# Hybrid encoder layer with a mixture of experts: units of the second expert loaded into tiles that the mix stage leaves

## The reference

```
logits = hf @ w_router + b_router            # top 4 of 32, softmax over the 4
hm = xblk @ w_mlp1[e] + b_mlp1[e]            # 1024 x 2048 weights
act = gate * sigmoid(1.702 * gate) * (up + 1)  # gate and up are clamped
y = act @ w_mlp2[e] + b_mlp2[e]              # 1024 x 1024 weights
x = x + sum over the chosen experts of weight * y ; out = rmsnorm(x, g_final)
```

## Time and profile of the kernel before

| what | us |
|---|---|
| three executions, median (lowest to highest) | 1252.73 (1252.02 to 1252.94) |
| the profiled execution, its own time | 1250.43 |
| its span, first to last instruction | 1248.6 |
| TensorE busy (93% of the span) | 1164.3 |
| VectorE, ScalarE, GpSimd busy | 361.7, 196.0, 23.8 |
| chain that ended last: TensorE, DMA | 55%, 41% |
| bytes moved | 445.25 MB, mean 357 GB/s |

### The profile page before, as it was taken

The page is one execution under the profiler, slowest core; times in us unless marked ns, Lnnn a source line. Parts: engine busy times, 40 slices in busy tenths (PEclk is TensorE's granted clock), DMA queues, the critical chain, the costliest instruction groups (busy, mean ns, idle before and its releaser), DMA issues.

```text
span 1248.6 us, 17054 instructions
## 1 busy us (share of the span) xinstructions
PE 1164.3 (93%) x6731; PEld 583.3 (47%) x6731; DVE 361.7 (29%) x1018; ACT 196.0 (16%) x383; POOL 23.8 (2%) x35
## 2 busy tenths in 40 slices
PE   9999999999999999989998989989899989999996
PEld 7888888889433333333333333333333333333332
DVE  4505788121522212212221222122222222222112
ACT  2121344001311011111101000100110111010002
POOL 0001011000000000000000000000000000000000
PEclk9999999999899999999999999999999999999999
DMA  9944323447699999999999999999999999999995
GB/s 310 311 135 135 105 98 102 173 147 290 252 416 430 426 428 427 427 428 428 428 428 428 428 429 428 429 428 428 428 428 428 428 428 429 429 428 427 427 426 231
DMA packets 69555, 445.25 MB, mean 357 GB/s; under 512 B 6247, under 2 KB 43595, under 8 KB 44651
## 3 DMA queue, kind: packets, MB, share of 16 engines
q1 hardware_dynamic: 65976, 441.99, 86.2%
q10 hardware_dynamic: 3539, 2.69, 0.7%
HBM read 443.62 MB, written 1.05 MB: 356 GB/s over the span
## 4 chain that ended last, share of the span: by engine, by line
PE 55%; DMA 41%; ACT 1%; issue 1%; DVE 1%; ACTq 0%; SPq 0%; POOL 0%; DVEq 0%
DMA ring<-in_w_mlp_dram 41%; PE bank L735 25%; PE bank L483 14%; PE bank L486 4%; PE bank L730 3%; PE bank L717 2%; PE bank L782 1%; PE bank L615 1%; PE bank L605 1%; PE bank L459 1%; PE bank L577 1%; PE bank L645 1%; ACT arena L1070 1%; PE bank L724 1%; PE bank L706 0%
## 5 line engine op out<-in xcount | busy, mean ns | idle before, releaser
L735 PE MATMUL bank<-ring,arena 128*64 128x512 f32 x3072 | 689.0, 597 | 56.8 <-DMA ring<-in_w_mlp_dram 55.1
L735 PEld LDWEIGHTS bank<-ring,arena 128*64 128x64 f32 x3072 | 209.6, 137 | 487.1 <-issue 367.9
L1448 DVE TENSOR_TENSOR arena<-bank,b1T 128x256 f32<-128x256 f32 x128 | 53.8, 421 | 599.6 <-PE bank L782 597.3
L483 PE MATMUL bank<-hT,ring 128*128 128x256 f32 x544 | 119.4, 379 | 0.0
L483 PEld LDWEIGHTS bank<-hT,ring 128*128 128x128 f32 x544 | 103.2, 190 | 14.0
L1067 ACT ACTIVATE arena<-bank 128x512 f32<-128x512 f32 x32 | 19.1, 597 | 362.3 <-PE bank L735 362.2
L730 PE MATMUL bank<-arena 64*128 64x512 f32 x256 | 63.6, 615 | 0.8 <-ACT arena L1079 0.8
L486 PE MATMUL bank<-ring,hT 128*128 128x256 f32 x288 | 63.8, 380 | 0.0
L486 PEld LDWEIGHTS bank<-ring,hT 128*128 128x128 f32 x288 | 54.2, 190 | 7.1
L717 PEld LDWEIGHTS bank<-slotP,hb 128*128 128x128 bf16 x1488 | 45.1, 98 | 23.5 <-issue 23.5
L782 PE MATMUL bank<-cst,arena 128*128 128x128 f32 x256 | 40.5, 286 | 13.2 <-ACT arena L1067 8.4
(11 more groups left out here) (229 smaller groups left out, 659.7 us busy)
## 6 DMA issues: line engine op xcount, KB each, us to landing
ring<-in_w_mlp_dram SPq DMA_DIRECT2D x190, 2048.0 KB, 32.7
ring<-in_w_in_dram SPq DMA_DIRECT2D x24, 1024.0 KB, 11.5
ring<-in_w_br_attn_dram SPq DMA_DIRECT2D x4, 1024.0 KB, 5.0
ring<-in_w_br_ssm_dram SPq DMA_DIRECT2D x4, 1024.0 KB, 5.1
ring<-in_w_out_dram SPq DMA_DIRECT2D x4, 1024.0 KB, 5.2
ring<-in_w_mlp_dram SPq DMA_DIRECT2D x4, 1024.0 KB, 33.9
xres<-in_x_dram SPq DMA_DIRECT2D x2, 512.0 KB, 4.5
cst<-shape_constants_dram ACTq DMA_DIRECT2D x1, 608.0 KB, 13.1
```

The source lines that it names most:

```text
L483: last = nc.tensor.matmul(o, w[:, k, a * P:(a + 1) * P], rhs[:, k, :], start=(k == 0), stop=(k == KD - 1))
L735: return nc.tensor.matmul(bank[b][side * CAP:(side + 1) * CAP, :], tokens, w, start=start, stop=stop, skip_group_check=True)
L1448: step(V.tensor_tensor(o, side(bank[b][:, :]), bias_h.to_broadcast([P, 4, CAP]), ALU.add))
```

## The change

Four units of the second expert, numbers 16 to 19 (its fifth to eighth), go to tiles outside the ring: 16 to `mix_only` (a new name for 8 KB per partition over constants and small tiles of the mix stage, which are put side by side for it), 17 to `hN`, 18 to `hT`, 19 to `xres`. `hb3` leaves `hT` for the arena. The two pairs after them (units 20 to 23) take the ring's first two places and are loaded as single units, each after its own slot's use. The first gather is cut in three: two tokens' slices, two more, and the other four between the second and third unit. Bias products and the token weights' transposes go from expert 0 to expert 28, all residual rows into the first expert and before it, g_final is loaded as one row and spread by a product with ones in expert 29, a one-column sigmoid stands ahead of ScalarE's loop, the last slot transposes move between up units, and each token tile is stored by one 512 KB transfer.

```diff
@@ tiles
+        mix_only = sb("mix_only", [P, UNIT], at=place_of["cst"] + 4 * C_GE)
...
+        gfin = arena[:, 2048:3072]
+        b2s = arena[0:NE, 2048:3072]
+        grow = arena[NE:NE + 1, 2048:3072]
+        hb3 = sb("hb3", [P, TT, D], BF16, at=place_of["arena"] + 4 * 3584)
+        lastWT = arena[:, 9536:9792]
+        AWAY = {16: mix_only[:, :], 17: hN[:, :, :].rearrange("p t d -> p (t d)"),
+                18: hT[:, :, :].rearrange("p k l -> p (k l)"), 19: xres[:, :, :].rearrange("p t d -> p (t d)")}
+HALVED = (PAIRS + 2, PAIRS + 3)
+        def turn(g, first):
+            return g - 2 if g >= PAIRS or not first else g
+        def pair_at(g, first=False):
+            return PAIR_ORDER[turn(g, first) % PAIRS]
@@ SP's queue
+            sp.wait_ge(y_psum, KD)
+            load_away(16)
+            for g in range(PAIRS):
+                first_free(pair_at(g, True))
+                load_first(g)
+            sp.wait_ge(unit_done, N_MIX)
+            load_away(18)
+            sp.wait_ge(lg_psum, 1)
+            load_away(17)
+            for g in HALVED:
+                p = pair_at(g, True)
+                for h, done in ((0, pair_full[p]), (1, half_full[HALVED.index(g)])):
+                    unit_used(sp, 0, 2 * (turn(g, True) - PAIRS) + h)
+                    sp.dma_start(ring[:, 2 * p + h, :], half_src(g // EXP_PAIRS, g % EXP_PAIRS, h)).then_inc(done, 16)
+            for g in range(HALVED[-1] + 1, BODY * EXP_PAIRS):
+                t = turn(g, True) - PAIRS
+                unit_used(sp, 0, 2 * (t + (2 if t >= PAIRS else 0)) + 1)
+                load_first(g)
+                if t == KD // 2 - 1:
+                    sp.wait_ge(rows_done, 1)
+                    sp.wait_ge(hb_ready, 1)
+                    sp.wait_ge(res_ready, 1)
+                    sp.wait_ge(away_full, 16 * 3)
+                    load_away(19)
...
+            for t in range(TT):
+                sp.wait_ge(fin_ready[2 * t], 1)
+                sp.wait_ge(fin_ready[2 * t + 1], 1)
+                sp.dma_start(out[0, t * P:(t + 1) * P, :], hN[:, t, :]).then_inc(out_done, 16)
@@ TensorE
             rows_in_sums(1, 1)
+            rows_in_sums(2, 0)
...
+            def first_expert():
+                pe.wait_ge(pw_ready, 1)
+                for q in range(KD):
+                    if q in (0, 2):
+                        pe.wait_ge(x0_ready, 1 + q // 2)
+                    if q == 2:
+                        first_gather(4, KD, 3).then_inc(x_psum, 1)
+                    if q == 4:
+                        pe.wait_ge(x32_ready, 1)
+                    up_unit(0, 0, q, body0=True)
+                rows_in_sums(2, 1)
+                pe.wait_ge(hs_ready, 1)
+                transposes(0).then_inc(t_psum, 1)
+                pe.wait_ge(hs_ready, 2)
+                transposes(1).then_inc(t_psum, 1)
+                pe.wait_ge(route_ready, 1)
+                rows_in_sums(3, 0)
+                rows_in_sums(3, 1).then_inc(rows_done, 1)
+                pe.wait_ge(hb_ready, 3)
+                pe.wait_ge(p_ready, 2)
+                gather(1, 3).then_inc(x_psum, 1)
+                down_units(0, 0, body0=True)
...
+            def expert(i, c, final=False, body0=False, bias_too=False, gain_too=False):
...
+                    if bias_too and q == 1:
+                        pe.wait_ge(late_in, 16 * 3)
+                        weights_T()
+                    if bias_too and q in (3, 5):
+                        bias_products(q // 4)
+                    if gain_too and q in (1, 3):
+                        gain_rows(q // 2)
+                    if final and q == 5:
+                        slot_transposes(c % 2, 3).then_inc(pw_psum, 1)
...
+            pe.wait_ge(p_ready, 1)
+            first_gather(0, 2, 3).then_inc(x0_psum, 1)
+            first_gather(2, 4, 2).then_inc(x0_psum, 1)
+            first_expert()
@@ ScalarE
-            act.wait_ge(wT_psum, 1)
-            nc.scalar.activation(wT[:, :], bank[6][0:NE, 0:SEQ], ACT.Copy).then_inc(wT_ready, 1)
...
-            act.dma_start(gfin, g_final.partition_broadcast(P)).then_inc(gfin_in, 16)
+            nc.scalar.activation(stat[:, 24:25], stat[:, 40:41], ACT.Sigmoid)
+            act.dma_start(b2s, b_mlp2[0]).then_inc(late_in, 16)
+            act.dma_start(grow, g_final).then_inc(late_in, 16)
...
+                for h in range(2 if gain_too else 0):
+                    act.wait_ge(gain_psum, h + 1)
+                    nc.scalar.activation(gfin[:, h * 512:(h + 1) * 512], bank[3][:, :], ACT.Copy, scale=float(D) ** 0.5).then_inc(gfin_ready, 1)
...
-                act.dma_start(out[0, t * P:(t + 1) * P, 512:1024], fin(hN, q)).then_inc(out_done, 16)
@@ VectorE
+            dve.wait_ge(x0_psum, 1)
+            first_tokens(0, 2, 3).then_inc(x0_ready, 1)
+            dve.wait_ge(x0_psum, 2)
+            first_tokens(2, 4, 2).then_inc(x0_ready, 1)
             first_residual(0)
-            first_tokens(1, x_psum).then_inc(x32_ready, 1)
             first_residual(1).then_inc(res_ready, 1)
+            dve.wait_ge(x_psum, 1)
+            first_tokens(4, KD, 3).then_inc(x32_ready, 1)
```

More of the change, by code:

```diff
@@ L798, in expert @@
-            def expert(i, c, first=False, final=False, rows_too=False):
-                e = i * BODY + c
-                pe.wait_ge(pw_ready, e + 1)
-                if first:
-                    pe.wait_ge(x0_half, 1)
-                else:
-                    pe.wait_ge(x32_ready, e + 1)
-                for q in range(KD):
-                    if first and q == 4:
-                        pe.wait_ge(x32_ready, e + 1)
-                    up_unit(i, c, q, final)
-                    if rows_too and q % 2 == 1 and q // 2 >= 2:
-                        add_rows(q // 2)
-                for b in range(2):
-                    pe.wait_ge(hs_ready, 2 * e + (b + 1))
-                    transposes(b).then_inc(t_psum, 1)
-                if first:
-                    bias_products()
-                    pe.wait_ge(hb_ready, 3)
-                else:
-                    pe.wait_ge(ys_ready, e)
-                    for q in range(4):
-                        combine(q)
-                if not final:
-                    pe.wait_ge(p_ready, e + 2)
-                    gather((c + 1) % 2, 3).then_inc(x_psum, 1)
-                else:
-                    slot_transposes(c % 2, 3).then_inc(pw_psum, 1)
@@ new lines, in weights_T, with bias_products @@
+            def weights_T():
+                for t in range(TT):
+                    last = nc.tensor.transpose(bank[3][0:NE, t * P:(t + 1) * P], wtok[:, t, 0:NE], ident)
+                last.then_inc(wT_psum, 1)
+            def bias_products(t):
+                pe.wait_ge(wT_ready, 1)
+                for hf in range(2):
+                    nc.tensor.matmul(bank[SUMS + 2 * t + hf][:, :], wT[:, t * P:(t + 1) * P],
+                                     b2s[:, hf * 512:(hf + 1) * 512], start=False, stop=False, skip_group_check=True)
```

199 lines of the change are left out of this document (106 added, 93 removed).

## The result

| | before | after |
|---|---|---|
| median of the runs, us | 1252.59 (1252.02 to 1252.94, 4 runs) | 1240.13 (1239.74 to 1242.50, 4 runs) |
| profiled execution: own time, span | 1250.43, 1248.6 | 1240.16, 1238.4 |
| its mean granted clock | 0.996 | 0.998 |
| forecast for after | | 1245.4, range 1241.2 to 1249.7 |

The ratio of the medians is 0.9909 [0.9895, 0.9924]: 11.4 us faster (12.5 by the two medians), where 7.3 were forecast. Between the two profiled executions it is 10.3 us, inside the 10 to 12.7 of rival A.

The account below looks back on a forecast made before the run. The weight stream at the DMA's 428 GB/s ceiling bounds the kernel, so idle DMA time before it becomes unbroken counts. 6.9 + 0.2 + 0.2 = 7.3 us off the median 1252.73 gives 1245.4 us, range 1241.2 to 1249.7.

Parts of the forecast that it names:

- rival A: Queue decides, not unit 21, if the clock does not fall at 316: gain 10 to 12.7 us, 1240 to 1243; 20%.
- step (3): First gather split: low clock stays, 0.5 us charged for the swap, 0.4 credited, eighth unit still ends at 335.8.
- g18: MoE pair load number 18, counted from 0, waiting for unit 21: its bytes were to begin at 371.6, before 378.5.
- Step (5): Transposes, bias products, gain rows moved to experts 28 and 29: some 4.0 and 1.8 us, free within TensorE's slack.
- (1): Units 16 to 18 loaded outside the ring, in idle queue time: 7.3 us of stream moved ahead.
- (2): First refills as single units, each on its own use: SP's four issues instead of two are hidden, cost nothing.
- (6): Stall moves: about 5.8 us of new idle near 366 to 371, ended by unit 21; gain 6.9 us, not 12.7.
- (7): Tail: final slot transposes leave the chain, 0.2 us; two 512 KB stores in place of four, 0.2 us gained.
- B: TensorE slower in the first expert, table load staying or low clock twice as long: 1246.5, 1248.7, both 1249.8; 17%.
- C: Slower: low clock held from 316 for more than 21 us, past the first expert's units; 1257 at 30 us; 3%.
- D: A wait in SP's queue holds the half loads and extra units land late: gain less than 2.5 us; 4%.

Follow-up runs that it names:

- experiment 1: After, with one row product (0.43 us) moved from ahead of the first gather to behind expert 0's eighth up unit: 1242.88 us, 0.9923.
- experiment 3: The kernel before, unchanged, profiled a second time: 1253.1 us, mean clock 0.993.
- experiment 11: The kernel before, its four 32-row bias products replaced by 128-row products of the same length (b_mlp2 left out of the result): 1250.08 us, 0.9987.
- 2: The kernel before, with one scratch row product of 256 columns added ahead of the gather: 1250.70 us, 0.9988.
- 9: After, with both halves of the first gather whole again ahead of unit 0: 1239.65 us, 0.9909.
- experiment 10: The kernel of experiment 6, its extra products given 32 rows of contraction instead of 128: 1246.19 us, 0.9958.
- experiment 4: After without tiles outside the ring, units 16 to 19 loaded into the ring as single units: 1245.73 us, 0.9946.
- experiment 8: After, with units 17 and 18 loaded later, next to unit 19; second form, without the wait ahead of unit 19: 1243.39 us, 0.9932.
- experiment 6: After, with four unread 128-row products of 512 columns added behind unit 7, ahead of the gather: 1244.62 us, 0.9939.
- more single refills: After, with the two pairs that refill the slots of units 20 to 23 loaded unit by unit: 1240.01 us, 0.9905; second run 1239.64 us, 0.9903.

## Why the prediction was wrong, and where it was right

**The step that failed is (3).** It said that the clock is at 1.2 GHz from 316.25 to 322.90 "after two short waits of TensorE, and those waits remain", so that the eighth unit ends where it did, at 335.8. Of the two waits, the one ahead of the gather did not remain: the change's own row product fills its 0.43 us, which step (3) leaves out and rival A names. And where that wait was put back (experiment 1), the clock stayed up in the profile all the same. In after the clock is full all the way, and the gather and units that step (3) had at the low level take 2.1 us for half a gather and 1.8 for a unit. The eighth unit ends at 332.1, 3.7 us before the forecast; 0.44 of that is an earlier end of the mix stage, which no part of the change makes. Unit 8 starts at 335.86 against 339.8, unit 21's use is at 365.8 against 369.7, g18's bytes at 367.5 against 371.6: the same 4 us all the way. That is the condition of rival A, with the sizes that it gave (3.2 us more, g18 at 368.4, 1240 to 1243).

What ends the fall? It came in all three profiles with the gather whole and no row product ahead of it (before, experiments 3 and 11); in none with a row product added (2, 9, and after itself), and not with a split gather alone (1). Either edit seems enough, but each alone rests on one or two profiles, and how the chip decides stays open.

**A second error lies ahead of the steps.** The prediction took one execution at a mean clock of 0.996 for the kernel, and set the 2.3 us up to the median aside as "what executions differ". In experiment 3 an execution near the median has a second fall, on and behind the bias products, and with it g18 is issued 2.8 us later. Step (5) moved these products as "free" and priced only their own 3.6 us. The stretch of full clock behind them was a gain no step had. Experiments 10 and 11 point to the few rows of contraction; neither shows it by its times alone. By experiment 11 it is worth 1.8 us in the median, with the interval [-0.4, 3.6] from its ratio; by 10, 1.6 us by the medians, 2.4 by the two ratios (0.0019 of 1252) and 1.8 by g18's issue. The after kernel has the same products in experts 28 and 29, where TensorE has slack; no profile of it shows a fall there.

**The other steps.**
(1) Right: units 16 to 18 fill 314.6 to 319.5. The four are worth 3.5 to 5.1 us by themselves (4), 17 and 18 at most 2.8 of it and about 1.6 by the estimate (8), not 7.3: what is idle before is partly idle again at 364.6 to 367.5.
(2) Right: SP's four issues cost nothing. The single refills follow TensorE's use, which leaves the queue at 343 and 389 GB/s from 319.5 to 347.
(3) Besides the clock: the split was charged and credited about nothing, and no worth of it shows (9).
(5) Right for the moved work itself: the stream from 500 to 1200 us runs at 428 GB/s, and the last pair lands 10.04 us earlier, with the products behind it.
(6) Right in kind: the new gap is there, ended by the use of unit 21, and experiment 6 gives 3.6 us of time for 3.6 us of TensorE. It is 2.9 us long (364.6 to 367.5) and not 5.8, as TensorE was 4 us earlier and the queue 1.2 us earlier than computed. The 1.9 us from issue to bytes holds as a cost only: what the stream loses at a restart is 1.7 to 1.9 us, but bytes flow within the first microsecond, at a third of the rate for two (experiment 6). The restart moved 11.0 us by the reading of the bytes and the last pair 10.04; the 1 us between is not accounted for.
(7) From the last pair to the end, 28.9 us against 29.1: 0.2 gained where 0.4 were forecast.

So the sum, 7.3 us, is near what the kernels differ by at the same clock (7.1 at 0.998, 6.8 at 0.997, 8.1 by the lines), and the 3.4 to 4.7 us above it go with falls that after does not have. That agreement is in part luck: the sum has the first expert's fall in both kernels, and at an equal high clock neither has it. The forecast set the gain from the clock at zero and gave rival A one chance in five; the range took A in only to 11.5 us of its 12.7.

**Rivals.** A came by its condition (no fall at 316), its sizes and its time, but not by its title, that the queue decides and not unit 21: the gap near 366 is there, which the prediction gave as the sign against A, and experiment 6 has unit 21 decide. B is out (no loads, no longer fall). C is out: no fall in the first expert in any profile of after. D is out: the loads went out in the order computed, none behind a wait of SP that was not foreseen.

## What to carry to other kernels

Before a sum is set against one profile, look at the mean clock of all executions: where they spread (here 0.991 to 0.999, 1.0 us of time for each 0.001 by the line through before, 1.5 by after's), some lose a stretch that the profiled one did not, and a second profile shows where. Where TensorE's way to the first refill decides when a stream becomes unbroken, price each low-clock stretch on that way as a term of the sum, with both outcomes in the range. Products with few rows of contraction are best put where TensorE has slack: here they cost their own time and, it seems, often the clock behind them. When an edit that is to price one thing adds a wait, look at the trace for what the wait cost before the time is read.

## What the runs showed of the hardware that was not expected

- The clock fell with TensorE busy without a gap: behind 3.7 us of products with 32 rows it went to a granted 0.52 for 3.3 us, behind 3.6 us of products with 128 rows it stayed at 1.00 (experiment 10).
- Falls come by chance too. Six of the 18 profiles have one of about 3.5 us in the mix stage, at 10 to 15, 40 to 45 or 57 to 61 us, which moves all that follows by some 2 us (307.42 to 309.66 in experiment 1).
- An issue to an empty queue is answered at once, but slowly: with the queue at 20 GB/s over the 4 us before and g18 issued at 371.84, it moves 147 GB/s from 372 to 374 and 295 from 374 to 375 (experiment 6). What the stream loses by it is 1.7 to 1.9 us.
- Three waits of 2.0 to 2.1 us of TensorE for a load were each followed by a fall of about 3.5 us (granted 0.53 or 0.54) within 1 us: at 353.3 in experiment 8's second form of the late units, at 1185.1 in experiment 4 and at 1180.6 in the second run of more single refills. Between 300 and 1205 us no profile has another wait for a load above 1.3 us, and behind none of the shorter ones, some 40 in each profile, came a fall. The fall at 316 of the kernel before came behind two waits for VectorE of 0.46 and 0.43 us; the profile of experiment 1 has both and no fall there. What the fall costs at 353 was 0.8 and 1.0 us on two units of 1.89.
